# A fused two-block model kernel: its first turn rewritten

## What is computed

```python
mem_n = rmsnorm(mem, mem_norm_g)                 # 256 x 1024
h = rmsnorm(x, norm_g[0])                        # x * rsqrt(mean(x*x over the row) + 1e-6) * g
proj = h @ fox_w_in[0]                           # q, k, v, f_logit, q_mem, z
log_f = log_sigmoid(f_logit + b_f); c = cumsum(log_f, over tokens)
s = q k^T / sqrt(128) + c_query - c_key; causal mask; softmax; times v
o = concat(main, memory heads) * silu(z); x = x + o @ w_out[0]
```

## Time and profile before

| | |
|---|---|
| median of 3 runs | 1951.25 us (1951.1 to 1953.92) |
| the profiled execution | 1953.56 us, its span 1951.9 us |
| TensorE busy | 1881.8 us of the span |
| VectorE, GpSimd, ScalarE busy | 871.8, 763.2 and 722.1 us |
| granted TensorE clock, mean | 0.984 of full |
| start of the scores of head 0 | 80.54 us after the span's start |

### The profile page before, as it was taken

The page is one execution under the profiler, slowest core; times in us unless marked ns, Lnnn a source line. Parts: engine busy times, 40 slices in busy tenths (PEclk is TensorE's granted clock), DMA queues, the critical chain, the costliest instruction groups (busy, mean ns, idle before and its releaser), DMA issues.

```text
span 1951.9 us, 24796 instructions
## 1 busy us (share of the span) xinstructions
PE 1881.8 (96%) x8567; PEld 1524.9 (78%) x8567; DVE 871.8 (45%) x1523; ACT 722.1 (37%) x1119; POOL 763.2 (39%) x365
## 2 busy tenths in 40 slices
PE   6799999999999999999999999998999899999997
PEld 4677887788887777878878888867788678888885
DVE  3433333343223434333239999936333354545213
ACT  4332333333244444433333233236233354444222
POOL 2444434444343333344434433323344434444441
PEclk8899999999999999999999999999999999999998
DMA  4223333333332222233323333312233323333332
GB/s 136 81 76 91 86 86 81 86 90 102 89 108 87 88 85 86 79 94 86 97 86 97 110 85 87 77 44 70 85 93 105 90 65 97 97 97 97 93 97 70
DMA packets 330996, 173.44 MB, mean 89 GB/s; under 512 B 16455, under 2 KB 327147, under 8 KB 330936
## 3 DMA queue, kind: packets, MB, share of 16 engines
q1 hardware_dynamic: 317088, 163.14, 29.5%
q0 software_dynamic: 2976, 9.32, 1.7%
q10 hardware_dynamic: 10872, 0.19, 0.3%
HBM read 170.42 MB, written 2.20 MB: 88 GB/s over the span
## 4 chain that ended last, share of the span: by engine, by line
PE 91%; DVE 4%; ACT 2%; DMA 2%; issue 1%; SPq 0%; ACTq 0%; DVEq 0%
PE proj L1664 27%; PE proj L1666 26%; PE proj L1665 26%; PE PV L1760 1%; PE A L1728 1%; DVE A L1346 1%; PE PV L1764 1%; PE A L1734 1%; PE A L1744 1%; PE A L1815 1%; PE PV L1815 1%; DMA wraw<-fox_w_in 1%; DMA wraw<-w_in 1%; PE A L1822 1%; PE A L1806 1%
## 5 line engine op out<-in xcount | busy, mean ns | idle before, releaser
L457 POOL TENSOR_TENSOR wlo<-wraw,whi 128x1024 fp32r<-128x1024 f32 (+2 forms) x307 | 722.5, 2356 | 1107.2 <-ACT whi L559 1107.1
L1664 PE MATMUL proj<-Hh,whi 128*128 128x512 f32 x1704 | 693.5, 407 | 15.7 <-DVE q L1162 10.0
L1666 PE MATMUL proj<-Hh,wlo 128*128 128x512 f32 x1704 | 668.0, 392 | 0.0
L1665 PE MATMUL proj<-Hl,whi 128*128 128x512 f32 x1704 | 667.2, 392 | 0.0
L559 ACT ACTIVATE whi<-wraw 128x1024 fp32r<-128x1024 f32 (+2 forms) x306 | 318.8, 1043 | 771.6 <-DMA wraw<-fox_w_in 202.2
L1664 PEld LDWEIGHTS proj<-Hh,whi 128*128 128x128 f32 x1704 | 322.8, 189 | 92.8 <-issue 19.1
L1665 PEld LDWEIGHTS proj<-Hl,whi 128*128 128x128 f32 x1704 | 322.7, 189 | 75.1 <-issue 10.9
L1666 PEld LDWEIGHTS proj<-Hh,wlo 128*128 128x128 f32 x1704 | 322.0, 189 | 68.6
L1346 DVE SCALAR_TENSOR_TENSOR A<-cin,dwT,A 128x512 f32<-128x512 f32 x232 | 175.0, 754 | 6.8
L1664 PE MATMUL proj<-Oh,whi 128*128 128x512 f32 x256 | 101.1, 395 | 0.7 <-DVE Ol L1146 0.7
L1666 PE MATMUL proj<-Oh,wlo 128*128 128x512 f32 x256 | 99.7, 389 | 0.0
(11 more groups left out here) (306 smaller groups left out, 2220.4 us busy)
## 6 DMA issues: line engine op xcount, KB each, us to landing
wraw<-w_in SPq DMA_DIRECT2D x68, 512.0 KB, 3.7
wraw<-fox_w_in SPq DMA_DIRECT2D x57, 512.0 KB, 3.6
wraw<-ret_w_in SPq DMA_DIRECT2D x44, 512.0 KB, 3.7
wraw<-w_up SPq DMA_DIRECT2D x44, 512.0 KB, 3.7
wraw<-w_out SPq DMA_DIRECT2D x40, 512.0 KB, 3.9
wraw<-w_mem_kv SPq DMA_DIRECT2D x16, 512.0 KB, 3.8
wraw<-w_down SPq DMA_DIRECT2D x16, 512.0 KB, 3.9
wraw<-conv_pw_w SPq DMA_DIRECT2D x8, 512.0 KB, 3.9
```

What stands on the lines that cost most here:

```text
L457: pool.tensor_tensor(wlo[s][:, 0:r, :], wraw[s][:, 0:r, :], whi[s][:, 0:r, :].bitcast(F32), ALU.subtract).then_inc(w_lo, 1)
L1664: mm(dst, whi[s][:, c, :], xh, start=(first and c == 0), stop=False)
L1665: mm(dst, whi[s][:, c, :], xl, start=False, stop=False)
L1666: ins = mm(dst, wlo[s][:, c, :], xh, start=False, stop=(last and c == chunks - 1))
```

## The change

Only the first turn is rewritten; weights, products, and all that comes after the scores of head 0 stay as they are.

- **Loads.** All start loads are SyncE's, in this order: ident, the 16 rows of `norm_g`, columns 0 to 511 of x (one load, 1 MB), forget weights, columns 512 to 1023 of x, the weights of query, key and value, the memory rows, then 18 small ones (10 vectors, the forget bias, 2 bias tables, the convolution rows, 4 rows of feed-forward taps) and the mask; only then the gate block's weights.
- **x.** TensorE turns the 16 rows of `norm_g` first, then chunk c of x into a bank of its own for c up to 5 (`x_bank`: A0 to A3, VT, PV, A0, A1). Chunks 6 and 7 are turned after the forget block's chunks 0 and 1. VectorE copies chunks 0 to 5 to `X`, ScalarE chunks 6 and 7; `Hl` is made from the PSUM bank and no longer from `X`. ScalarE puts the high parts of the first weights between its `Hh`.
- **Row norm.** The 8 squares and the 8 `mean_d` matmuls go. ScalarE squares the four row tiles of `xin` as landed with an accumulated sum per row (128x1 each), makes rsqrt from 128x4 sums; VectorE multiplies the identity with them, and one `mean_d` matmul inside the key block (before chunk 3) spreads them to all partitions.
- **Forget and query side by side.** From chunk 2 on TensorE does three forget products of chunk c and two query products of chunk c-2; the query's eight `wlo` products come last.
- **Order behind.** q is evacuated as soon as `rms` is there, ahead of the forget chain. The full vectors, the bias rows and the tap rows are turned between key, value and gate blocks. Memory chunks 0 to 3 are turned inside the value block (before chunk 5), 4 to 7 inside the gate block (before chunk 4). GpSimd's b and c stores stand behind its splits of later blocks; ScalarE's and VectorE's parts are sorted to match.
- The tile `squared` goes, and two unused fillers shift where the start's tiles lie in SBUF.

```diff
+        x_bank = [*A, VT, PV, A[0], A[1]]
@@ sync
+            sp.dma_start(vrows[V_NORM:V_NORM + 16, :], rows_by(t["norm_g"].rearrange("a n -> (a n)"))).then_inc(in_const, 16)
+            for half in range(2):
+                at = slice(half * S, (half + 1) * S)
+                sp.dma_start(xin[:, :, at], rows_by(t["x"][0], "(a p) n -> p a n")[:, :, at]).then_inc((in_x, in_x_late)[half], 16)
+                if half == 0:
+                    load("forget", 0, 0)
+            for b in range(3):
+                load("fox", 0, b)
+            sp.dma_start(memin[:], rows_by(t["mem"][0], "(a p) n -> p a n")).then_inc(in_mem, 16)
...
@@ gpsimd
             for n in range(LO_AHEAD):
                 pool.wait_ge(w_hi, n + 1)
                 pool.tensor_tensor(wlo[n][:], wraw[n][:], whi[n][:].bitcast(F32), ALU.subtract).then_inc(w_lo, 1)
             split("forget", 0, 0)
@@ fox_turn(0), gpsimd
                 split("fox", i, 0)
                 split("fox", i, 1)
+                    pool.wait_ge(b_out, 2)
+                    pool.dma_start(b_dram, bias_rows[:]).then_inc(b_stored, 16)
...
@@ scalar
             logs()
+            first_hi(0)
+            act.wait_ge(taken0, 1)
+            for c in range(4):
+                first_h(c)
+            first_hi(1)
+            for c in range(4, X_DVE):
+                first_h(c)
+            first_hi(2)
+            for c in range(X_DVE, KC):
+                act.wait_ge(turned0, 2 + c)
+                f(X[:, c, :], x_bank[c][:], ACT.Copy).then_inc(x_done, 1)
+                first_h(c)
             split("forget", 0, 0)
...
+                f(memsq[:], xin[:, i, :], ACT.Square, accum_out=x_sums[:, i:i + 1]).then_inc(x_squared, 1)
+            own.mark(f(x_logs, x_sums, ACT.Ln, scale=1.0 / D, bias=EPS))
+            f(x_roots, x_logs, ACT.Exp, scale=-0.5).then_inc(x_rooted, 1)
+            split("fox", 0, 0)
...
@@ vector
+            arrived("forget", 0, 0)
+            dve.tensor_copy(f_x, proj[PH["forget"].bank(0)][0:HEADS, :]).then_inc(evac, 1)
+            dve.wait_ge(x_rooted, 1)
+            tt(sq[:].rearrange("p (a b) -> p a b", a=NT), ident[:].unsqueeze(1).broadcast_to([P, NT, P]),
+               x_roots.unsqueeze(2).broadcast_to([P, NT, P]), ALU.mult).then_inc(x_diag, 1)
+            dve.wait_ge(x_spread, 1)
+            ts(rms[:], A[3][:], float(D), None, ALU.mult).then_inc(rms_ready, 1)
+            arrived("fox", 0, 0)
+            stt(q[:], proj[fox.bank(0)][:], SCALE, rms[:], ALU.mult, ALU.mult).then_inc(evac, 1)
...
@@ tensor
+            for c in range(6):
+                turn_x(c)
+            pe.wait_ge(w_lo, 1)
+            forget_part(0)
+            turn_x(6)
+            forget_part(1)
+            turn_x(7)
+            pe.wait_ge(w_hi, 2)
+            for c in range(2, KC):
+                forget_part(c)
+                query_part(c - 2)
+            query_part(KC - 2)
+            query_part(KC - 1)
+            pe.wait_ge(w_lo, 2)
             for c in range(KC):
+                ins = mm(to_q, wlo[s_q][:, c, :], Hh[:, c, :], start=False, stop=(c == KC - 1))
+            ins.then_inc(w_used, 1)
...
+            def first_mem(c):
+                if c == 5:
+                    pe.wait_ge(mem_scaled, MT)
+                    pe.wait_ge(taken0, 2)
+                    pe.wait_ge(rms_ready, 1)
+                    for x in range(4):
+                        turn_mem(x)
+            products("fox", 0, 2, 2, H, each=first_mem)
```

More of the change, by code:

```diff
@@ L136, in build @@
         tops8 = small[:, 32:40]
+        x_sums, x_logs, x_roots = small[:, 48:52], small[:, 52:56], small[:, 56:60]
         with ExitStack() as begin:
@@ L422, in _ @@
                 if name == "fox":
-                    for b in range(4):
-                        load(name, 0, b)
+                    load(name, 0, 3)
                     with sp.Fori(1, TURNS[name]) as i:
@@ L609, in _ @@
             f(small[:, 24:26], small[:, 22:24], ACT.Exp, scale=-0.5).then_inc(mem_rms, 1)
[L610 to L612 removed]
+            split("fox", 0, 1)
             act.wait_ge(f_step, 2)
@@ L759, in wo_turn @@
                 wo_step(name, i, 1)
-            softmax_turn("fox", 0, 0, None)
+            split("fox", 0, 2)
+            act.wait_ge(taken0, 2)
+            for c in range(KC):
+                mem_high(c)
+            split("fox", 0, 3)
+            z_and_v("fox", 0, 0)
             softmax_turn("fox", 1, 1, "fox")
@@ L1064, in _ @@
[L1064 to L1075, removed]
@@ new lines, in _ @@
+            take_x(0)
+            take_x(1)
+            dve.wait_ge(taken0, 1)
+            for c in range(KC):
+                if c + 2 < X_DVE:
+                    take_x(c + 2)
+                first_low(c)
+            arrived("forget", 0, 0)
[3 more added lines that the diff above has]
+               x_roots.unsqueeze(2).broadcast_to([P, NT, P]), ALU.mult).then_inc(x_diag, 1)
@@ L1685, in square_in @@
-            def square_in(c):
-                pe.wait_ge(start_sq, c + 1)
-                ins = mm(VT[:], mean_d[:], (sq, squared)[c % 2][:], start=(c == 0), stop=(c == KC - 1))
-                ins.then_inc(start_sq_used, 1)
-                pe.wait_ge(h_ready, c + 1)
-            products("forget", 0, 0, 0, H, each=square_in)
-            products("fox", 0, 0, 0, H)
-            products("fox", 0, 1, 1, H)
-            pe.wait_ge(mem_scaled, MT)
-            for c in range(KC):
-                if c == 0:
-                    pe.wait_ge(x_done, KC)
-                if c >= 4:
-                    pe.wait_ge(mem_lo, c - 3)
+            pe.transpose(PV[:, 0:16], vrows[0:16, :], ident[0:16, 0:16]).then_inc(turned0, 1)
@@ new lines, in turn_x @@
+            def turn_x(c):
+                pe.wait_ge(in_x if c < 4 else in_x_late, 16)
+                if c == 5:
+                    pe.wait_ge(taken0, 1)
+                if c > 5:
+                    pe.wait_ge(h_ready, c - 5)
+                for i in range(NT):
+                    ins = pe.transpose(x_bank[c][:, i * P:(i + 1) * P], xin[:, i, c * P:(c + 1) * P], ident[:])
+                ins.then_inc(turned0, 1)
+            to_forget, to_q = proj[PH["forget"].bank(0)][:], proj[PH["fox"].bank(0)][:]
@@ new lines, in _, with spread_roots @@
+            query_part(KC - 2)
+            query_part(KC - 1)
+            pe.wait_ge(w_lo, 2)
+            for c in range(KC):
+                ins = mm(to_q, wlo[s_q][:, c, :], Hh[:, c, :], start=False, stop=(c == KC - 1))
+            ins.then_inc(w_used, 1)
+            def spread_roots(c):
+                if c == 3:
+                    pe.wait_ge(x_diag, 1)
+                    mm(A[3][:], mean_d[:], sq[:], start=True, stop=True).then_inc(x_spread, 1)
+            products("fox", 0, 1, 1, H, each=spread_roots)
@@ L1702, in _, with turn_mem @@
+            pe.wait_ge(in_vec, 16 * 11)
+            pe.transpose(A[2][:, 0:V_ROWS], vrows[:], ident[0:V_ROWS, 0:V_ROWS]).then_inc(turned0, 1)
+            pe.wait_ge(in_bucket, 16 * 7)
+            for x in range(2):
+                mm((VT, PV)[x][0:HEADS, 0:448], rb[:], hot[:, x * 448:(x + 1) * 448], start=True, stop=True).then_inc(b_made, 1)
+            def turn_mem(c):
                 for a in range(MT):
@@ L1716, in _, with last_mem @@
             ins.then_inc(turned0, 1)
-            pe.wait_ge(b_out, 2)
-            pe.wait_ge(taken0, 2)
+            def last_mem(c):
+                if c == 4:
+                    for x in range(4, KC):
+                        pe.wait_ge(mem_lo, x - 3)
+                        turn_mem(x)
+            products("fox", 0, 3, 3, H, each=last_mem)
             def fox_scores(u):
```

163 lines of the change are left out of this document (94 added, 69 removed).

## The result

The changed kernel takes 1920.33 us (median of 4, 1918.92 to 1921.64) against 1952.59 (1951.1 to 1954.59) for the kernel before on the same chip: ratio 0.9834, 95% interval 0.9817 to 0.9851. The forecast was 1924, the range 1920 to 1931.5. The profiled execution took 1918.92, its span 1917.2.

A forecast was written before the change was run, and what follows sets the result against it. TensorE, busy 1881.8 of 1951.9 us, was taken as the bound. The new start summed to 51.0 plus a stall of 1.1: scores at 52.1 instead of 80.54, 28.4 us earlier, so 1924 us, range 1920 to 1931.5.

The forecast's parts named there:

- The walk: Step-by-step sum of the new start up to head 0's scores: 51.0 without a stall, 52.1 with it, instead of 80.54 us.
- the sum's own bounds: Bounds on landing, clock and stall at the start: a gain of 22.4 to 30.1 us, total 1921 to 1931.5.
- rival 2: At the start: no stall, early clock, sooner landing; gain over 30.5 us, total below 1920; chance 5%.
- the signs: What the new trace should show in the first turn, such as first forget product at 14 to 16, scores at 50 to 58.
- The halt of 6.85 us: In the old start TensorE stops turning x at 17 and goes on at 23.84; the wait was called VectorE's.
- Landing: Start loads: x's first half at 6.8, forget weights 8.6, second half 12.4 (bounds to 14.2), query weights 14.2 us.
- Low clock: TensorE from 14.1: 5.4 us at low clock, 1.7 us lost (bounds 1.1 and 2.3).
- The stall of 1.1 us in the value block: TensorE at chunk 5 waits for the vectors at 41.0, GpSimd's subtraction holding VectorE's forget chain; bounds 0 to 4.7.
- Row norm, q, gate block, softmax: First-turn waits claimed hidden: row norm by 1.7 to 3 us, gate block by 1.9, softmax by 2.1; q's 10.05 goes.
- The masked row: GpSimd's mask row for head 0's softmax, expected last, at 54.7 us.
- Squares: Row norm at the start: one matmul pass of 0.86 us stands in for eight, 6.9 us.
- rival 3: SyncE's 20 loads ahead of the gate weights are held up; at 4.87 us each the kernel is 56 slower, 2007; chance 3%.

## Why the prediction was right, and where it was off

- **Direction and main mechanism** held: 31.35 of the spans' 34.7 us are won ahead of the scores of head 0, and from 11.63 on TensorE is the bound there without a wait. The walk gave 52.1; it was 49.19, reproduced at 49.00 and 48.91.
- **The range** held by little, and partly by luck. Its lower end was put at 1920 where the sum's own bounds gave 1921, and 1920.33 lies between them. The gain ahead of the scores, 31.35, is above the sum's upper bound of 30.1: what happened is rival 2 (no stall, an early clock, a sooner landing), which had 5%. Of the signs, the first forget product (13.25, not 14 to 16), the scores (49.19, not 50 to 58), the clock's return (16.2, not 18 to 21) and the gap of 1 us in the value block came out otherwise; `Hl` at 0.74 and the single `mean_d` matmul near 30 (28.60) as said. One of its signs of being wrong came true: the time from the scores to the end was 1868.0, not 1871.4. The forecast took that time as fixed; traces of the same work give 1868.0 to 1875.2.
- **The halt of 6.85 us** was read as VectorE's. VectorE was only its last link, with ScalarE's order and the landing of the key weights behind it. The walk through the new order had both right, so the sum didn't suffer.
- **Landing.** I took 12.4 for x's second half from the forget weights' row; its first transpose came at 11.63, and the first products 0.85 us earlier. The first half was right (6.8, measured 7.08 with the first transpose). Query weights, forecast for 14.2, were being copied at 13.38. That the halves are what buys it was overrated: only 0.6 to 0.9 us of the scores are theirs.
- **Low clock.** Taken as 1.7 us lost until 19.5; by the products' pace it ended near 16.2, so about 1.0 was lost, and chunk 7 turned in 0.44 instead of 0.85. The pace has to be used here: PEclk reads 1.00 from the start, also from 13 to 15 us, where the products come 0.43 apart.
- **The stall of 1.1 us in the value block** failed outright. It rested on GpSimd's subtraction for head 1's query block at 33.7 to 36.0. I counted one block too far: that subtraction stands behind the c store in GpSimd's order and ran at 44.15, after VectorE's chain. The only contention was 1.69 instead of 0.67 us in the chain's first instruction. Term: 1.1 forecast, 0 measured.
- **Row norm, q, gate block, softmax**: hidden, as said. The one matmul pass took 0.86 as taken, the diagonal was ready at 25.8 (27.3 forecast). The masked row was 50.15 instead of 54.7, by the same miscount.
- **Squares**: forecast 6.9 less 0.86; their return cost 6.6 to 6.8.
- **SyncE** (rival 3): its 20 loads were issued by 20.2 as reckoned, the memory rows' in 1.94 us, the small ones in 0.26 to 0.41 each, and the gate weights' issue waited for TensorE at 23.64.
- **Total.** 2.9 us of the 3.7 by which 1924 was high are the walk's: 0.85 for the landing, 1.0 for the low clock and the paces behind it, 1.1 for the stall. The remainder is within how far the rest varies from run to run.

## What to carry to other kernels

When the first stage of a kernel is short of work for its bound engine, several waits lie side by side: take one away alone and the next shows (4.1 us, then 3.2 behind the scores), so walk through the whole order before judging a part. Put evacuations that free the bound engine ahead of long serial chains, and follow the chain on to its last consumer, through every engine that hands it on. Follow a wait back as well: the engine that ended it may itself have waited. And price a wait with its clock: 4.5 us of idling cost 6.5.

## What was not expected of the hardware

Behind waits of 1.9 and 1.4 us a few us apart TensorE's clock was low, and in another version it was low (0.50) behind small matmuls with no wait over 0.43 us. The same wait in the same place (2.7 us, near 750 us behind the scores) left a stretch of 10 us at 0.66 in the kernel before, at 0.83 in seven traces of the others (in one of them the next stretch) and at 1.00 in five. Traces of the same work behind the scores differ by up to 7 us, more than the gain of most single edits here; the clock goes with part of that, and is not shown to be its cause. And transposes alone raised the clock: with x whole, the pace of the sixteen and eight transposes quickened at 13.3 us, 3.4 us after the first, without one product before them. It doesn't always come so soon: the kernel before made 24 in 5.12 us without it.
